# Returned rows added to x by GpSimd on landing instead of by VectorE in two late steps, in a float32 decoder trunk on one Trainium2 core

## What is computed

```python
for e in range(N_EXPERTS):
    out = out + swiglu(t, w_gate[e], w_up[e], w_down[e]) * gates[:, e:e + 1]
x = x + out
return rms_norm(x, final_norm_g)
```

## Time and profile before

| what | value |
|---|---|
| median of 3 runs | 1398.28 us (1398.0 to 1399.54) |
| the profiled execution's own time | 1398.18 us |
| its span, first to last instruction | 1396.3 us |
| PE busy, of the span | 1369.0 us (98%) |
| DVE busy | 1152.0 us (83%) |
| ACT busy | 972.1 us (70%) |
| POOL busy | 121.0 us (9%) |
| granted TensorE clock, mean | 0.996 |

### The profile page before, as it was taken

How to read it: one execution, slowest core, us unless ns; L and a number is a source line. 1 busy time by engine, 2 the same in 40 slices (tenths; PEclk the granted TensorE clock), 3 DMA queues, 4 the chain that set the end, 5 groups by cost and what they waited for, 6 DMA issues and landing times.

```text
span 1396.3 us, 17620 instructions
## 1 busy us (share of the span) xinstructions
PE 1369.0 (98%) x6701; PEld 1141.0 (82%) x6701; DVE 1152.0 (83%) x948; ACT 972.1 (70%) x883; POOL 121.0 (9%) x45
## 2 busy tenths in 40 slices
PE   9999999999999999999999999999999999999997
PEld 8888788888888787888888888878888878787786
DVE  6556355555578769999999999989999989998997
ACT  5444435443365756888888888878888878878885
POOL 1000001000000001000100610100510100420000
PEclk9999999999999999999999999999999999999999
DMA  9745454555554337999999999999999999999993
GB/s 379 291 158 176 176 190 158 195 195 181 175 170 168 121 122 275 412 426 417 426 414 426 428 428 428 425 406 427 419 430 427 425 410 427 420 428 427 427 422 128
DMA packets 40308, 453.24 MB, mean 325 GB/s; under 512 B 4481, under 2 KB 4609, under 8 KB 8353
## 3 DMA queue, kind: packets, MB, share of 16 engines
q1 hardware_dynamic: 37264, 440.85, 78.1%
q0 software_dynamic: 2816, 11.18, 2.1%
q10 hardware_dynamic: 144, 0.09, 0.0%
HBM read 445.55 MB, written 6.55 MB: 324 GB/s over the span
## 4 chain that ended last, share of the span: by engine, by line
PE 71%; DVE 14%; DMA 7%; issue 6%; ACT 2%; POOL 0%; DVEq 0%; SPq 0%; ACTq 0%
PE psum L1923 16%; PE psum L1925 16%; PE psum L1924 16%; PE psum L2288 7%; PE psum L2289 7%; DVE w_lo L1314 7%; DVE w_lo_last L1314 3%; DMA work<-in_moe_w_down 3%; PE psum L2341 2%; ACT w_hi L922 2%; DMA raw<-in_moe_w_gate 1%; DMA raw<-in_moe_w_down 1%; PE psum L1969 1%; PE psum L1970 1%; PE psum L1971 1%
## 5 line engine op out<-in xcount | busy, mean ns | idle before, releaser
L1314 DVE TENSOR_TENSOR w_lo<-raw,w_hi 128x2048 fp32r<-128x2048 f32 (+1 forms) x294 | 659.2, 2265 | 149.4 <-ACT w_hi L922 148.6
L922 ACT CAST w_hi<-raw 128x2048 fp32r<-128x2048 f32 (+1 forms) x294 | 556.4, 1895 | 196.7 <-PE psum L1925 135.9
L1923 PE MATMUL psum<-w_hi,actA_hi 128*128 128x512 f32 (+1 forms) x648 | 254.6, 393 | 2.4 <-DVE actA_lo L1680 0.8
L1925 PE MATMUL psum<-w_hi,actA_lo 128*128 128x512 f32 (+1 forms) x648 | 249.5, 385 | 0.0
L1924 PE MATMUL psum<-w_lo,actA_hi 128*128 128x512 f32 (+1 forms) x648 | 248.9, 384 | 0.0
L2288 PE MATMUL psum<-w_hi,actB_hi 128*128 128x512 f32 x444 | 178.0, 401 | 3.6 <-DVE actB_hi L1684 2.2
L2289 PE MATMUL psum<-w_lo,actB_hi 128*128 128x512 f32 x444 | 174.6, 393 | 0.0
L1923 PEld LDWEIGHTS psum<-w_hi,actA_hi 128*128 128x128 f32 x648 | 121.9, 188 | 27.3 <-DVE w_lo L1314 2.0
L1925 PEld LDWEIGHTS psum<-w_hi,actA_lo 128*128 128x128 f32 x648 | 121.7, 188 | 24.9
L1924 PEld LDWEIGHTS psum<-w_lo,actA_hi 128*128 128x128 f32 x648 | 122.0, 188 | 22.6
L1923 PE MATMUL psum<-w_hi,actB_hi 128*128 128x512 f32 x300 | 118.2, 394 | 0.8 <-DVE w_lo L1314 0.8
(11 more groups left out here) (276 smaller groups left out, 1992.9 us busy)
## 6 DMA issues: line engine op xcount, KB each, us to landing
raw<-in_moe_w_gate SPq DMA_DIRECT2D x42, 2048.0 KB, 12.1
raw<-in_moe_w_up SPq DMA_DIRECT2D x42, 2048.0 KB, 12.1
raw<-in_moe_w_down SPq DMA_DIRECT2D x42, 2048.0 KB, 12.4
work<-in_moe_w_up SPq DMA_DIRECT2D x14, 2048.0 KB, 12.4
work<-in_moe_w_gate SPq DMA_DIRECT2D x14, 2048.0 KB, 12.3
work<-in_moe_w_down SPq DMA_DIRECT2D x14, 2048.0 KB, 11.3
raw<-in_ret_w_in SPq DMA_DIRECT2D x22, 1024.0 KB, 9.9
raw<-in_ffn_w_gate SPq DMA_DIRECT2D x11, 1024.0 KB, 4.9
```

Of the source, the lines that this page charges most:

```text
L922: nc.scalar.copy(hi_of(u)[:, 0:size], raw_of(w, u)[:, 0:size]).then_inc(sem["hi_ready"], 1)
L1314: nc.vector.tensor_tensor(lo_of(u)[:, 0:size], raw_of(w, u)[:, 0:size], as_f32(hi_of(u)[:, 0:size]), ALU.subtract).then_inc(sem["lo_ready" ...
L1923: nc.tensor.matmul(dst, l_hi[:, k, cols], r_hi[:, kk, rcols], start=first, stop=False)
L1925: return nc.tensor.matmul(dst, l_lo[:, k, cols], r_hi[:, kk, rcols], start=False, stop=last)
```

## The change

GpSimd, which has issued the load of `y_back` and would next do `root("final")`, now waits for that load (`y_in`) and does the four additions itself, one row of two per token and tile at a time, with the same operands, the same `comb` increments and the same wait between the first and the second addition to a tile. VectorE's `expert_step` loses them. VectorE's wait for `comb` to be 4 before `combined` stays.

```diff
@@ -902,6 +902,12 @@
             pool.sem_inc(sem["back_asked"], 1)
             pool.dma_start(y_back.rearrange("p t k d -> p t (k d)"),
                            y_dram[P:, :].rearrange("(t p k) d -> p t (k d)", t=TILES, k=2)).then_inc(sem["y_in"], 16)
+            pool.wait_ge(sem["y_in"], 16)
+            for k in range(2):
+                for t in range(TILES):
+                    if k:
+                        pool.wait_ge(sem["comb"], t + 1)
+                    nc.gpsimd.tensor_tensor(x[:, t, :], x[:, t, :], y_back[:, t, k, :], ALU.add).then_inc(sem["comb"], 1)
             root("final")
@@ -1813,13 +1819,6 @@
                 if n == 4 and at == "pair":
                     choose(w.column(1), 1)
                     rest_of_current(w.column(1))
-                if n >= STEPS - 2 and at == "last":
-                    k = n - STEPS + 2
-                    for t in range(TILES):
-                        dve.wait_ge(sem["y_in"], 16)
-                        if k:
-                            dve.wait_ge(sem["comb"], t + 1)
-                        nc.vector.tensor_tensor(x[:, t, :], x[:, t, :], y_back[:, t, k, :], ALU.add).then_inc(sem["comb"], 1)
                 split_to(7)
                 short_product(at, n - 1)
                 split_to(8)
```

## The result

The changed kernel takes 1400.12 us (median of 11 runs, 1398.47 to 1403.2) against 1398.28 us for the kernel before (11 runs beside them, 1396.15 to 1401.92). The ratio is 1.0017, with a 95% interval of 1.001 to 1.0025. So the change costs about 0.1 to 0.25%, 1.84 us by the medians. I had forecast 1397.8 us, half a microsecond less than before. The measured time lies inside my range, and the change is under 0.2%, but it is clear of noise and goes the other way. The profiled executions differ by 2.2 us of span (1398.5 and 1396.3).

A forecast was written before the change was run, and what follows sets the result against it. VectorE, late in the last pair with the loads close behind, was taken to bound the end: 4.75 us of stalls less 0.70 idle and 4.54 removed gave -0.5 us, so 1397.8 us, range 1395.5 to 1403.2.

The forecast's parts named there:

- the floor: Last pair: however much time VectorE is given, the loads let only about 2.1 us come back.
- The rival that the floor breaks: Last pair: loads issued earlier also land earlier, so all 4.54 us come back, to 1393.8 us; chance 0.10.
- The removed term: VectorE's queue in the last pair: four additions taken away, together 4.54 us by distance of starts.
- the sum: VectorE's delay less 0.70 us idle before 1294.54 us and 4.54 us removed; the rest reaches the end: -0.5 us.
- The added term: Four GpSimd additions from 1258.65 us hold VectorE's splits, 4.75 us in all.
- h: Time a GpSimd addition holds VectorE's next split after getting in: assumed 1.85 us, twice 0.92 for one input stream.
- the first hold: First GpSimd addition starts at 1258.65 us, VectorE's next split at 1260.37, so 1.72 us of its hold is hidden.
- S: Sum of the four holds on VectorE's splits, 4h - 2.65: 4.75 us with h = 1.85.
- my own mark of 420: Sign: loads issued under 9 us before landing in 1270 to 1300 us, and GB/s below 420, refute that loads stand the delay.
- the 1382: Sign at the end: a last VectorE split later than 1382 us means a hold above 2.5 us.
- Long holds: Rival: GpSimd holds VectorE for its whole instruction, 3.62 us or more; 1401 to 1407 us, slower, chance 0.19.
- The starved GpSimd: Rival: splits make GpSimd's additions wait and drag on at no cost; 1396.2 us, chance 0.22 together with small stalls.

The follow-up runs named there:

- e1_none: Kernel before with the four additions left out on every engine, GpSimd only counting `comb` up by 4: 1395.92 against 1397.97 us.
- e5_filled_all: Changed kernel plus extra TensorE matmuls in its three gaps, those in the middle gap adding zeros: +2.71 us against the kernel before, ratio 1.0018.
- the spread kernel: Changed kernel with only GpSimd's first addition at the landing, the others after the ends of steps 3, 4 and 5: +0.08 us against before, ratio 1.0005.
- e2_extra_two: Kernel before, additions kept on VectorE, plus four GpSimd additions doubling the returned rows at their landing: +2.43 us, ratio 1.0016.
- e9_pool_pairs: Changed kernel with two GpSimd additions at the end of step 3 and two at the end of step 4: +3.3 us against before, one run.

## Why the prediction was wrong

**What bounds, and the floor: right.** The additions stood on the path (TensorE's two waits above), and e1_none brought back 2.05 us where I had a floor of 2.1. The rival that the floor breaks and all 4.54 us come back is refuted by the same run.

**The removed term: mis-sized.** I credited the sum with 4.54 + 0.70 us, as if VectorE's backlog were all. The kernel after won 3.35 us in the two steps, since TensorE takes 29.5 us a step with no wait at all; the step of my sum that failed is "after that nothing is idle, and the rest arrives at the end". I had seen that TensorE lacked only 1 to 2 us of full in each window and drew no bound from it. The earlier trace rows allowed one: 1.85 + 0.88 = 2.7 us of TensorE idle in the two windows after 1294 us, 0.3 us a gap too little.

**The added term: mechanism right, size wrong.** GpSimd and the splits exclude each other, instructions with a PSUM operand go free, and the places were those I named. But h was 2.20 us in place of 1.85, and 0.59 us of the first hold was hidden in place of 1.72, as VectorE's split was ready at 1258.67 us in this execution. With these the formula gives 3 x 2.20 - 0.93 + 1.61 = 7.3 us, and the trace 7.35, where I had 4.75. That less of the first hold was hidden cost no time by itself: in e5_filled_all all but 0.07 us of it was hidden, the stretch was 5.84 us, and the step was as long. This leaves h. With 2.20 in my own formula S is 6.15 us and the sum 6.15 - 5.24 = +0.9 instead of -0.5. So the assumed hold is the failed step that turned the sign: twice the one-input hold was no measurement. The Trainium skill's 1.96 times VectorE's duration (GPSIMD Engine Reference, section 3.1), which I set beside the sum, gave an estimated 2.39 us. The trace agrees with it as the length of the unhindered addition, 2.406 us; the hold of 2.20 lies between it and my 1.85, and nearer to it. That this figure led to 1400.0 us, next to the measured 1400.12, is luck in part, as it stood beside the same credit of 5.24.

**Two errors that nearly cancel.** With the stretch of the trace my sum would have given 7.35 - 5.24 = +2.1 us, close to the +2.2 of span. That is luck. TensorE lost 5.89 of the 7.35 us, as VectorE's first split began 1.4 us earlier there than before (5.73 us after the marker in place of 7.13), and won 3.35 of the 5.24.

**The loads.** I said that they stand a delay. A block issued at 1275.90 us took 8.1 us, and the window 1274 to 1278 us moved about 140 GB/s, under my own mark of 420. TensorE did not wait for it: at full DMA rate after 1294 us the loads caught up while VectorE was behind. So the statement was wrong as to the rate and right as to the time.

**The signs.** The splits were stretched to about 4 us where I had said, and the last one began at 1379.4 us, under the 1382 that would have meant a hold above 2.5. But VectorE was not without idle time after 1294 us: it waited 1.6 us for ScalarE after 1320 us, 0.9 of it after 1340. I had written that this would mean that the loads are the bound. They were not: ScalarE was itself waiting for TensorE there, and for no load.

**Rivals.** Long holds of 3.62 us or more did not occur, though GpSimd's records were 4.4 us long. The starved GpSimd did occur, but only in the spread kernel, and there it did not end at 1396.2 us, because each of the last three holds still cost 1.9 us (1397.74 us measured).

## What to carry to other kernels

GpSimd is no free helper beside a VectorE that is busy with two SBUF inputs: a 128x1024 float32 addition that costs VectorE 1.13 us itself costs it 2.2 us when GpSimd does it (GpSimd's unhindered 2.4 us less 0.2), less what an idle VectorE or one with a PSUM operand hides. When two engines are nearly as busy (28.3 and 29.5 us a step here), extra work cost nothing here as long as each step of the lighter engine stayed within the heavier one's; spreading the four additions one to a step, on the same engine, gave 0.9983 of the time, which beats both kernels. And a credit for removed work is to be capped by the next engine's idle time in the same windows before it goes into a sum.

## What the runs showed of the hardware that was not expected

- How long GpSimd holds VectorE off by the inputs, 1024 columns each: 0.83 us for one, 1.69 for two that are the same row, 2.20 for x and a returned row, and 1.10 for 512 columns of these. The shortest records beside them are 2.79, 1.88, 2.41 and 1.29 us. So with two inputs the hold is the unhindered instruction less 0.2 us, with one it is less than a third of the record. Why the two differ is open.
- A lone GpSimd addition waited 15 us behind splits that followed one another, while one right behind another got in at the next boundary. The rule is open.
- TensorE's granted clock fell to its lower level for 3.4 us at 1272.4 us in the kernel after, behind gaps of 1.9, 2.3 and 2.3 us, and at 1263.7 us in e2_extra_two, behind one gap of 2.8. It stayed up in e5_filled_all, where the gaps were filled, and also in e9_pool_pairs behind gaps of 1.4 and 2.3 us. Between the kernel after and e5_filled_all it made no difference in time, as TensorE was waiting for splits.
